# Main attention with tokens sorted by parity inside each tile of 128, dilated branches packed by key tile

## The reference

```python
BRANCHES = ((128, 1), (512, 4), (2048, 16))   # window, dilation
q = rope((x @ w_q).reshape(B, S, 3 * 16, 64)); k = rope(...); v = ...   # k, v from kv_norm(h) @ w_kv
for g, (window, dilation) in enumerate(BRANCHES):
    o, lse = dilated_branch(q[:, :, g], k[:, :, g], v[:, :, g], window, dilation)
    # query t attends to t, t-d, t-2d, ..., t-window; never ahead of itself
wts = softmax(stack(lses)); o = sum over branches of wts * o; y = o @ w_o
```

## Time and profile before

| | |
|---|---|
| median of 3 runs | 1091.74 us |
| profiled execution, span | 1089.5 us |
| the same as a run's time | within the 1090.97 to 1091.83 of the runs |
| TensorE matmul, weight load | 1082.7 us (99%), 980.4 us (90%) |
| VectorE, ScalarE, GpSimd | 814.4 us (75%), 657.3 us (60%), 54.3 us (5%) |
| main attention steps | about 301.7 to 548.2 us |

### The profile page before, as it was taken

The page is one execution under the profiler, slowest core; times in us unless marked ns, Lnnn a source line. Parts: engine busy times, 40 slices in busy tenths (PEclk is TensorE's granted clock), DMA queues, the critical chain, the costliest instruction groups (busy, mean ns, idle before and its releaser), DMA issues.

```text
span 1089.5 us, 18377 instructions
## 1 busy us (share of the span) xinstructions
PE 1082.7 (99%) x6900; PEld 980.4 (90%) x6900; DVE 814.4 (75%) x1217; ACT 657.3 (60%) x976; POOL 54.3 (5%) x47
## 2 busy tenths in 40 slices
PE   8999999999999999999999999999999999999998
PEld 8998888888899999889888888889999989999987
DVE  5986878785688787877768878735796787899970
ACT  6546755464588778777766546544555656666650
POOL 0000000000000000000000000000200111222300
PEclk9999999999999999999999999999999999999999
DMA  8565665776386545542447566762444663655760
GB/s 264 184 199 174 220 201 175 249 253 191 101 219 200 167 137 163 156 134 76 131 129 232 175 210 215 267 195 88 144 148 134 198 224 121 193 178 181 236 235 20
DMA packets 214410, 193.86 MB, mean 178 GB/s; under 512 B 8089, under 2 KB 189773, under 8 KB 214349
## 3 DMA queue, kind: packets, MB, share of 16 engines
q1 hardware_dynamic: 213993, 192.81, 56.6%
q10 hardware_dynamic: 356, 0.22, 0.1%
HBM read 191.95 MB, written 1.05 MB: 177 GB/s over the span
## 4 chain that ended last, share of the span: by engine, by line
PE 94%; DVE 2%; ACT 1%; DMA 1%; SPq 1%; issue 0%; DVEq 0%; ACTq 0%
PE ps L795 13%; PE ps L644 8%; PE ps L645 8%; PE ps L646 8%; PE ps L699 7%; PE ps L700 7%; PE ps L701 7%; PE ps L871 7%; PE ps L799 7%; PE ps L872 3%; PE ps L815 2%; PE ps L816 2%; PE ps L817 2%; PE ps L894 1%; PE ps L921 1%; PE ps L908 1%
## 5 line engine op out<-in xcount | busy, mean ns | idle before, releaser
L1808 DVE TENSOR_TENSOR w_lo<-raw,w_hi 128x1024 fp32r<-128x1024 f32 (+1 forms) x298 | 398.1, 1380 | 53.2 <-ACT w_hi L1312 52.3
L1312 ACT ACTIVATE w_hi<-raw 128x1024 fp32r<-128x1024 f32 (+1 forms) x298 | 331.4, 1156 | 115.2 <-PE ps L701 37.7
L644 PE MATMUL ps<-x_both,w_hi 128*128 128x256 f32 x656 | 186.8, 285 | 0.2 <-DVE w_lo L1808 0.2
L646 PE MATMUL ps<-x_both,w_lo 128*128 128x256 f32 x656 | 185.6, 283 | 0.0
L645 PE MATMUL ps<-x_both,w_hi 128*128 128x256 f32 x656 | 185.6, 283 | 0.0
L795 PE MATMUL ps<-x_both,w_hi 128*128 128x512 f32 x640 | 153.1, 391 | 0.0
L795 PEld LDWEIGHTS ps<-x_both,w_hi 128*128 128x128 f32 x640 | 117.6, 188 | 23.5 <-DVE w_lo L1808 0.7
L644 PEld LDWEIGHTS ps<-x_both,w_hi 128*128 128x128 f32 x656 | 125.8, 192 | 1.7 <-issue 1.3
L645 PEld LDWEIGHTS ps<-x_both,w_hi 128*128 128x128 f32 x656 | 125.9, 192 | 0.0
L646 PEld LDWEIGHTS ps<-x_both,w_lo 128*128 128x128 f32 x656 | 125.8, 192 | 0.0
L699 PE MATMUL ps<-w_hi,a_hi 128*128 128x512 f32 x296 | 115.7, 391 | 0.0
(11 more groups left out here) (255 smaller groups left out, 1828.4 us busy)
## 6 DMA issues: line engine op xcount, KB each, us to landing
raw<-in_ffn_w_gate_up SPq DMA_DIRECT2D x80, 512.0 KB, 5.1
raw<-in_w_up SPq DMA_DIRECT2D x44, 512.0 KB, 4.5
raw<-in_ffn_w_down SPq DMA_DIRECT2D x24, 768.0 KB, 5.9
raw<-in_conv_w_in SPq DMA_DIRECT2D x24, 512.0 KB, 5.3
raw<-in_w_q SPq DMA_DIRECT2D x48, 256.0 KB, 4.6
raw<-in_w_kv SPq DMA_DIRECT2D x48, 256.0 KB, 4.1
raw_v<-in_w_kv SPq DMA_DIRECT2D x48, 256.0 KB, 3.4
raw<-in_w_in SPq DMA_DIRECT2D x20, 512.0 KB, 4.5
```

What stands on the lines that cost most here:

```text
L644: nc.tensor.matmul(o, wh[:, k0 + k, c], hi[:, k, :], start=(k == 0), stop=False)
L646: ins = nc.tensor.matmul(o, wl[:, k0 + k, c], hi[:, k, :], start=False, stop=(k == kt - 1))
L1312: nc.scalar.activation(w_hi[:, s, a * ph.cols:b * ph.cols], src, ACT.Copy)\
L1808: nc.vector.tensor_tensor(w_lo[:, s, c], src, w_hi[:, s, c], ALU.subtract)\
```

## The change

Tokens are now sorted by parity *inside* each tile of 128: tile 0 is its 64 even tokens and then its 64 odd ones, tile 1 likewise. A *class* is one of the two parities, 64 tokens of a tile.

- **Scores.** Query tile 0 needs only key tile 0 (128 local columns), query tile 1 all 256. For the dilated branches each class of queries meets only keys of its own class: blocks of 64 queries x 64 keys. Class 0 writes its rows with branch 1 in the first 64 columns of a block and branch 2 in the next 64, class 1 the other way round. Each product now covers a quarter of the array (64 rows x 64 columns). 32 products in place of 12. A head has 768 columns of probabilities in place of 1024: 256 for query tile 0 and 512 for tile 1.
- **Probabilities.** 12 transposes in place of 16 (`PROB_TURNS`); the maximum, the exponential, the scaling and ScalarE's copy (1536 columns in place of 2048) shrink with them.
- **Values.** After the transposition a block has 64 keys of one branch in the low half of the partitions and 64 keys of the other branch in the high half. So `v_tok` holds three blocks of 128 columns: local values in order; branch 1 low and branch 2 high for class 0; branch 2 low and branch 1 high for class 1. `store_v` has four instructions on 64 partitions each in place of one on 128; two of the four write to the other half. `value` has 12 products with other sizes; the last of them also waits for `roped`, and `score` no longer does.
- **Sorting.** The order is made where the normed activations are written before the attention (`high` on ScalarE and `low` on VectorE for the boundary `bi == 2`), in the positions, and in the row of norms; rope writes and value projection are plain. `store_y` undoes it.
- The mask has 768 columns in place of 1024.

The core of the diff (left out: the same renaming in other places, the mask's construction):

```diff
-        rparity = small[:, 42:44]
+        rclass = small[:, 42:44]
+        HEAD_P = 768
+        PROB_TURNS = ((0, 0), (P, 2 * P), (2 * P, P), (3 * P, 4 * P), (4 * P, 3 * P), (5 * P, 5 * P))
...
-                    if parity:
-                        high, low = by_parity(hi[:, k, :])[:, t, :], by_parity(lo[:, k, :])[:, t, :]
-                    else:
-                        high, low = hi[:, k, tok(t)], lo[:, k, tok(t)]
+                    high, low = hi[:, k, tok(t)], lo[:, k, tok(t)]
...
                 def score():
                     if isinstance(i, int) and i == 1:
                         pe.wait_ge(v_stored, 1)
-                    pe.wait_ge(roped, q * 3 + 3)
+                    if second:
+                        pe.wait_ge(roped, q * 3 + 3)
                     for qt in range(2):
-                        for g in range(3):
-                            k = slice(0, T) if g == 0 else tok(qt)
+                        own = P * (qt + 1)
+                        for c in range(CLASSES):
                             for hh in range(2):
...
+                                nc.tensor.matmul(flat[m, o0:o0 + own], qkT[f, 0, q0:q0 + CB], qkT[f, 3, 0:own], start=True,
+                                                 stop=True, skip_group_check=True)
+                        for kt in range(qt + 1):
+                            for n in range(2):
+                                for c in range(CLASSES):
+                                    for hh in range(2):
+                                        f, m = slice(hh * HD, (hh + 1) * HD), slice(c * CB, (c + 1) * CB)
+                                        g, q0, k0 = 1 + (n + c) % 2, qt * P + c * CB, kt * P + c * CB
+                                        o0 = S_AT + hh * 1024 + qt * 512 + own + kt * P + n * CB
+                                        ins = nc.tensor.matmul(flat[m, o0:o0 + CB], qkT[f, g, q0:q0 + CB],
+                                                               qkT[f, 3 + g, k0:k0 + CB], start=True, stop=True,
+                                                               skip_group_check=True)
...
-                def value(q):
+                def value(q, ropes=None):
...
+                    for kt in range(2):
+                        for hh in range(2):
+                            f, p0, w = slice(hh * HD, (hh + 1) * HD), hh * HEAD_P + kt * 4 * P, T - kt * P
+                            nc.tensor.matmul(flat[f, O_AT + kt * P:O_AT + T], v_tok[:, kt, f], prob[:, p0:p0 + w],
+                                             start=(kt == 0), stop=False, skip_group_check=True)
+                    for c in range(CLASSES):
+                        for hh in range(2):
+                            f, p0 = slice(hh * HD, (hh + 1) * HD), hh * HEAD_P + 2 * P
+                            v0 = (c + 1) * P + hh * HD
+                            nc.tensor.matmul(in_tiles(flat[f, O_AT:O_AT + T])[:, :, c, :], v_tok[:, 0, v0:v0 + HD],
+                                             in_tiles(prob[:, p0:p0 + T])[:, :, c, :], start=False, stop=False,
+                                             skip_group_check=True)
+                    for c in range(CLASSES):
+                        for hh in range(2):
...
+                            if ropes is not None and (c, hh) == (CLASSES - 1, 1):
+                                pe.wait_ge(roped, ropes)
+                            ins = nc.tensor.matmul(flat[f, o0:o0 + CB], v_tok[:, 1, v0:v0 + HD], prob[:, p0:p0 + CB],
+                                                   start=False, stop=True, skip_group_check=True)
...
             def high(bi, t, r, k):
+                if bi == 2:
+                    dst, src = in_classes(dst), classes(src)
...
-                    nc.vector.tensor_scalar(v_tok[:, t, :], ps[:, v_bank, 0:384], rparity[:, t:t + 1], None, ALU.mult)\
-                        .then_inc(v_stored if t else va_stored, 1)
+                    low, high = slice(0, HD), slice(HD, P)
+                    ends = v_tok[high, t, :].rearrange("p (g c) -> p g c", c=P)[:, 0:3:2, :]
+                    first_two = ps[high, v_bank, 0:2 * P].rearrange("p (g c) -> p g c", c=P)
+                    nc.vector.tensor_scalar(v_tok[low, t, 0:2 * P], ps[low, v_bank, 0:2 * P], rclass[low, t:t + 1], None, ALU.mult)
+                    nc.vector.tensor_scalar(v_tok[high, t, P:2 * P], ps[low, v_bank, 2 * P:3 * P], rclass[low, t:t + 1], None,
+                                            ALU.mult)
+                    nc.vector.tensor_scalar(ends, first_two, rclass[high, t:t + 1], None, ALU.mult)
+                    nc.vector.tensor_scalar(v_tok[low, t, 2 * P:3 * P], ps[high, v_bank, 2 * P:3 * P], rclass[high, t:t + 1], None,
+                                            ALU.mult).then_inc(v_stored if t else va_stored, 1)
```

More of the change, by code:

```diff
@@ L446, in build, with classes, in_classes, tiles @@
         rcol = small[:, 50:52]
-        rparity = small[:, 42:44]
-        def by_parity(t):
-            return t.rearrange("p (b c) -> p c b", c=2)
+        rclass = small[:, 42:44]
+        HEAD_P = 768
+        PROB_TURNS = ((0, 0), (P, 2 * P), (2 * P, P), (3 * P, 4 * P), (4 * P, 3 * P), (5 * P, 5 * P))
+        def classes(t):
+            return t.rearrange("p (b c) -> p c b", c=CLASSES)
+        def in_classes(t):
+            return t.rearrange("p (c b) -> p c b", c=CLASSES)
+        def tiles(t):
+            return t.rearrange("p (t b c) -> p t c b", t=2, c=CLASSES)
+        def in_tiles(t):
+            return t.rearrange("p (t c b) -> p t c b", t=2, c=CLASSES)
         def by_token(t):
@@ L801, in gated_blocks, with token_major @@
                 return ins
-            def token_major(ph, j, t, bank, hi, lo, signal=0, tile=None, done=product_done, parity=False):
+            def token_major(ph, j, t, bank, hi, lo, signal=0, tile=None, done=product_done):
                 s = (ph.n0 + j) % 4
@@ L853, in turn_probs, with turn_classes @@
                 ins.then_inc(prob_turned, 1)
-            def turn_parity():
+            def turn_classes():
                 pe.wait_ge(col_set, 2 * 2 + 2)
                 for t in range(2):
[L859 to L862, removed]
+                    for c in range(CLASSES):
+                        ins = nc.tensor.matmul(ps[c * CB:(c + 1) * CB, 7, T + t:T + t + 1], classes(ident[:])[:, c, :],
+                                               rcol[:, t:t + 1], start=True, stop=True, skip_group_check=True)
+                ins.then_inc(classes_turned, 1)
             def feature_tile(ph, j, g, bank, both):
@@ L975, in attn_step @@
                     row(2)
[L976 removed]
+                    turn_classes()
                     turn_raw(0)
                     turn_raw(1)
[L979 to L980 removed]
+                    token_major(ph, 2, 0, banks[4], x_hi, x_lo, signal=1, done=tile_done)
+                    token_major(ph, 2, 1, banks[5], x_hi, x_lo, signal=2)
                 elif tail:
[L982 removed]
+                    value(q - 1, ropes=q * 3 + 3)
                     score()
@@ L1001, in attn_step @@
                     else:
-                        value(q - 1)
+                        value(q - 1, ropes=q * 3 + 3)
                         score()
@@ L2501, in additive, with own, packed @@
         return m[0:P, 0:P], m[P:T, 0:T]
-    by_parity = np.arange(T).reshape(T // 2, 2).T.reshape(T)
-    parts = [np.where((k <= q) & (q - k <= w) & ((q - k) % d == 0), 0.0, NEG).astype(np.float32)[by_parity][:, by_parity]
+    by_class = np.arange(T).reshape(2, CB, CLASSES).transpose(0, 2, 1).reshape(T)
+    parts = [np.where((k <= q) & (q - k <= w) & ((q - k) % d == 0), 0.0, NEG).astype(np.float32)[by_class][:, by_class]
              for w, d in BRANCHES]
-    mask3 = np.concatenate([p[c, 0:T] if g == 0 else p[c, c] for c in (slice(0, P), slice(P, T))
-                            for g, p in enumerate(parts)], axis=1)
+    def own(t, c):
+        return slice(t * P + c * CB, t * P + (c + 1) * CB)
+    def packed(qt, c):
+        return np.concatenate([parts[1 + (n + c) % 2][own(qt, c), own(kt, c)] for kt in range(qt + 1) for n in range(2)], axis=1)
+    mask3 = np.concatenate([m for qt in range(2) for m in (
+        parts[0][qt * P:(qt + 1) * P, 0:(qt + 1) * P], np.concatenate([packed(qt, c) for c in range(CLASSES)]))], axis=1)
     mask1 = np.concatenate(additive(k <= q), axis=1)
```

106 lines of the change are left out of this document (48 added, 58 removed).

## The result

| | before | after |
|---|---|---|
| median | 1092.0 us (11 runs) | 1094.34 us (1093.53 to 1095.85, 11 runs) |
| after to before | | 1.0022, 95% interval 1.0014 to 1.0030 |
| profiled execution, span | 1089.5 us | 1092.3 us |

The forecast was 1089.7 us, 2.0 us less than before; it became 2.3 us more. All 22 executions of the changed kernel (a second set gave 1093.56 us, ratio 1.0012, 1.0003 to 1.0021) have a median of 1094.2.

A forecast was written before the change was run, and what follows sets the result against it. TensorE was taken as the bound, busy 99% of the span. First step +1.44, six steady steps -4.80, last step +1.23 and norm +0.10 sum to -2.0 us: 1089.7 us, range 1088.7 to 1090.7.

The forecast's parts named there:

- A: Scores: the array's quarters take turns in pairs, scores 2.74 us, +5.0 us in all, 1096.8; chance 0.08.
- B: Scores: TensorE's instruction supply becomes the bound at 36 ns a record, +10.9 us, 1102.6; chance 0.13.
- the store: Value store on VectorE: four instructions one after another, 1.68 us, in place of one of 0.61.
- C: Value stores: writing across partitions is dear, 2.37 us a store, +4.9 us, 1096.6; chance 0.08.
- D: Value stores: VectorE's instructions overlap as now, 1.41 us a store, -4.9 us, 1086.8; chance 0.15.
- the two stores in front of the first scores: First step with scores: both stores precede the scores, 3.38 us in place of 1.14, so +2.24.
- output projection: Last step: the output projection waits for both stores and starts at 536.74 against 534.66, +2.08 us.
- norm stride: Norm before the attention: the stride moved there costs +0.1 us in all, bounds 0 and 0.7.
- value projection: Value projection: its weights are now dense instead of read with a stride, which changes nothing.
- A steady step -0.80, six of them (pairs 2 to 7): Main attention: -0.36 and -0.44 (transposes) shorten each steady step, -4.80 us over six.
- all the rest is projection: Steady step: beyond values, scores and transposes TensorE's stream is projection, 25.2 us of the step.
- something unseen: Whole kernel: the chance left for an outcome outside the forecast and the named rivals, 0.10.

The follow-up runs named there:

- e1: The kernel before, unchanged and run again: 1092.55 us, ratio 1.0003.
- e5: The kernel after, unchanged and run again: 1093.56 us, ratio 1.0012 to before.
- e9: The kernel after with 14 transposes of the probabilities in place of 12, two more that nobody reads: 1096.12 us.

## Why the prediction was wrong, step by step

- **Right, to 0.1 us:** values 1.49 (forecast 1.48), transposes 1.31, scores on four quarters at once (rivals A and B are out), the store 1.74 (1.68; rivals C and D are out), the projection held by the fourth store and 3.52 behind the values (3.48 forecast), the two stores in front of the first scores +2.30 (+2.24), output projection +2.11 (+2.08), norm stride 0 (+0.10), value projection 0. That the first scores also come +2.25 later than in `e1` is partly luck: 0.15 of it is the start, and counted from the products with `small` they are 1.8 to 2.4 us later, by which two traces one compares. By the Trainium skill's 62 ns per matmul ("TensorE: Matmul & The Clock Gate", "Wait — 56ns, not 53.3ns?") 32 products of scores would take 2.0 us, an estimate; the trace has them start within 1.36, 43 ns a product (two records), directly behind a wait too, so it doesn't bind here.
- **Failed: "A steady step -0.80, six of them (pairs 2 to 7)".** Five are steady. In step 2 VectorE comes late to its store, 2.9 us behind the values' start in place of 1.7 and with no idle time in front, so its longer store is not covered: +0.56 in place of -0.80. I had read the idle time of the store from a steady step alone; the first turn of the loop has the same code and other neighbours. 1.36 us.
- **Failed: "all the rest is projection".** I held its 25.2 us for a constant. It is not: the pace of 48 pairs changed from 0.347 to 0.353, +0.32 a step, 1.6 of the 1.70 us over five. Why it changes stays open. No row of before showed that it could. It puts the steady step at 30.30, outside the 29.6 to 30.2 by which I wanted to tell that I was wrong in kind.
- **Not priced: the waits of TensorE in the first and the last step.** I counted their length (right) but not that the granted clock falls behind them, 0 of 22 executions at 1.000 against 43 of 53. 0.7 to 1.3 us in the median, by filling them; 2.4 us in the trace of `e5`, in which it fell at both.

None of the rivals A to D came true; this was the "something unseen", to which I gave 0.10.

Sum: -2.0 + 1.36 + 1.70 - 0.3 (smaller terms) = +0.8, or +0.6 without the start, and 0.7 to 1.3 for the clock: +1.3 to +2.1, measured +2.3 (all runs: +2.1). What is left is not assigned; the starts of the executions alone lie up to 2.9 us apart.

## What to carry to other kernels

Price a longer instruction on a side engine in every kind of step, the first turn of a loop and the last one too: read there how late that engine is. A wait of TensorE can cost more than its length, when the granted clock falls behind it (here waits of 2.3 to 2.9 us), so look at the mean clock of all executions, not only at the profiled one. Before you compare two traces, look how far apart they are where the code is still the same. And a change that cuts TensorE's work into small blocks pays for the shuffling elsewhere: here it lost 2.1 us with all of it on VectorE, and won 6.9 with half of it on ScalarE.

## What the runs showed of the hardware

- fp32 products on quarters of the array (64 rows x 64 columns) run four at a time: 64 records start within 1.36 us, one every 22 ns on the mean.
- An instruction of VectorE on 64 partitions takes as long as one on 128 (0.47 to 0.48 us for 256 columns from PSUM, as in the earlier trace rows); its start is held until the end of the one before if it reads or writes in other partitions than that (0.49 to 0.51 us apart, otherwise 0.40 to 0.41). Writing across adds at most 0.01 us to its own duration.
- A run of projection matmuls keeps one of two paces, 0.347 or 0.353 us a pair, at the same granted clock (the slower repeats 0.349, 0.350, 0.361), mostly the slower behind 12 transposes (54 of 63) and the faster behind 16 (20 of 21).
- The same code in front of the change reaches the attention up to 2.9 us apart from execution to execution (306.68 to 309.62), up to 1.7 us with no stretch of the lower clock in front of it (`e9`).
